# Expert gates laid out in memory by group of four expert tiles, stored in parts by SyncE from two blocks

## The reference, cut to what matters

```python
def peer(h, w_query, sub_keys, expert_u, expert_v):
    q = (hf @ w_query).reshape(T, PEER_HEADS, 2, PEER_HALF)
    scores = jnp.einsum('thcd,hcnd->thcn', q, sub_keys)
    ... # top 16 of each half, then of their sums: top_s, idx
    gates = jax.nn.softmax(top_s, axis=-1)
    u = expert_u[idx_b]
    act = jax.nn.gelu(jnp.einsum('thkd,td->thk', u, x_b))
    vv = expert_v[idx_b]
    return jnp.einsum('thk,thkd->td', g_b * act, vv)
```

## Time and profile before

| | us |
|---|---|
| median of 3 runs | 2877.3 (2871.14 to 2883.05) |
| the profiled execution | 2897.03 |
| its span, first to last instruction | 2895.3 |
| up stage with gates, about | 1000 to 1740 |
| up stage without gates, up to | 1930 |
| down stage | 1930 to 2895 |

### The profile page before, as it was taken

How to read it: one execution, slowest core, us unless ns; L and a number is a source line. 1 busy time by engine, 2 the same in 40 slices (tenths; PEclk the granted TensorE clock), 3 DMA queues, 4 the chain that set the end, 5 groups by cost and what they waited for, 6 DMA issues and landing times.

```text
span 2895.3 us, 42514 instructions
## 1 busy us (share of the span) xinstructions
PE 2689.3 (93%) x15119; PEld 2367.3 (82%) x15119; DVE 2324.9 (80%) x4258; ACT 1265.2 (44%) x2394; POOL 1077.8 (37%) x779
## 2 busy tenths in 40 slices
PE   7999776979998999999999999988999999999998
PEld 4888544768888999999999999986777777777777
DVE  3562477447889999999899776659999999999998
ACT  4211466222222499999898872222222222222222
POOL 0000000001114444444445665535555555555552
PEclk8999887989999999999999999999999999999999
DMA  6640000314348788989899999989999999999997
GB/s 225 235 169 12 10 0 16 130 73 136 114 133 281 270 313 302 340 301 329 285 330 336 378 379 370 367 303 369 377 389 388 385 384 388 363 387 389 383 376 260
DMA packets 310035, 794.35 MB, mean 274 GB/s; under 512 B 26592, under 2 KB 125568, under 8 KB 305792
## 3 DMA queue, kind: packets, MB, share of 16 engines
q0 software_dynamic: 110592, 402.70, 38.1%
q1 hardware_dynamic: 176832, 301.73, 29.6%
q10 hardware_dynamic: 22464, 88.09, 7.6%
HBM read 694.11 MB, written 98.30 MB: 274 GB/s over the span
## 4 chain that ended last, share of the span: by engine, by line
PE 36%; DVE 17%; DMA 12%; issue 9%; ACT 4%; SPq 1%; DVEq 0%; ACTq 0%
PE ps_up L392 29%; DVE row_sum L119 10%; DMA stage<-v_cols 8%; PE ps_g L439 4%; PE ps_y L802 3%; DMA expert_gate<-g_buf 2%; DMA stage<-expert_act 1%; DVE acc L856 1%; DVE coef_lo L877 1%; ACT key_distance L331 1%; DMA stage<-cols 1%; ACT v_hi L769 1%; DVE fetched L114 1%; ACT second_gate L335 1%; PE ps_g L407 1%
## 5 line engine op out<-in xcount | busy, mean ns | idle before, releaser
L96 POOL DMA_INDIRECT fetched<-u_rows,row_index x384 | 558.3, 1454 | 706.8 <-DVE row_act L114 588.5
L96 POOL DMA_INDIRECT fetched<-v_cols,row_index x384 | 515.4, 1342 | 423.4 <-DVE row_sum L119 367.8
L392 PE MATMUL ps_up<-h_hi,col_hi 128*128 128x320 f32 (+1 forms) x2288 | 555.1, 323 | 38.5 <-DVE col_lo L484 20.0
L392 PE MATMUL ps_up<-h_lo,col_hi 128*128 128x320 f32 (+1 forms) x2288 | 547.3, 320 | 0.0
L392 PE MATMUL ps_up<-h_hi,col_lo 128*128 128x320 f32 (+1 forms) x2288 | 546.7, 319 | 0.0
L114 DVE CUSTOM_DVE_ANT_0 fetched<-fetched,h_rows_then_gates 128x1024 f32<-128x1024 f32 x384 | 452.8, 1222 | 55.5 <-DMA fetched<-u_rows,row_index 42.3
L119 DVE SCALAR_TENSOR_TENSOR row_sum<-fetched,row_act,row_sum 128x1024 f32<-128x1024 f32 x381 | 486.8, 1278 | 1.5 <-DVE row_sum L119 0.5
L802 PE MATMUL ps_y<-v_hi,coef_hi 128*128 128x512 f32 x1280 | 406.0, 399 | 61.6 <-DVE coef_lo L877 57.1
L392 PEld LDWEIGHTS ps_up<-h_hi,col_hi 128*128 128x128 f32 x2288 | 387.8, 190 | 51.0 <-issue 35.2
L769 ACT ACTIVATE v_hi<-stage 128x1024 fp32r<-128x1024 f32 x128 | 135.9, 1062 | 647.9 <-DMA stage<-v_cols 638.1
L802 PE MATMUL ps_y<-v_lo,coef_hi 128*128 128x512 f32 x1280 | 400.6, 395 | 0.0
(11 more groups left out here) (245 smaller groups left out, 3487.3 us busy)
## 6 DMA issues: line engine op xcount, KB each, us to landing
stage<-cols SPq DMA_DIRECT2D x144, 512.0 KB
stage<-v_cols SPq DMA_DIRECT2D x128, 512.0 KB
expert_act<-stage ACTq DMA_DIRECT2D x128, 320.0 KB
expert_gate<-g_buf ACTq DMA_DIRECT2D x20, 2048.0 KB
stage<-expert_act SPq DMA_DIRECT2D x128, 320.0 KB
z_t<-w_ada SPq DMA_DIRECT2D x48, 512.0 KB, 6.1
g_raw<-expert_gate SPq DMA_DIRECT2D x64, 320.0 KB
h_rows_then_gates<-expert_gate SPq DMA_DIRECT2D x64, 320.0 KB
```

The source lines that it names most:

```text
L96: nc.gpsimd.indirect_dma_start(self.buf[:, n % NBUF], None, rows, bass.IndirectOffsetOnAxis(ap=self.at[:, tile, k:k + 1], axis=0)).then_in ...
L392: mm = pe.matmul(ps_up[:, b, half, 0:width], w[:, b, k], h[:, k, a:a + width], start=(k == 0 and i == 0), stop=(k == DC - 1 and i == 2))
```

## The change

`gate_d` becomes [32 groups, 128, 20 blocks, 4 tiles, 32 tokens]. A quarter's read in the down stage is now one stretch of 2560 bytes a partition, 128 pieces. A block's store writes 512 bytes at a stretch, 32 of them a partition, 4096 pieces for 2 MB.

The stores move from ScalarE's queue to SyncE's. Blocks of four groups alternate between `g_buf` and the columns of the gathered tokens in `h_hi` and `h_lo` (three blocks of 128 tokens, no longer read in the up stage), by way of plain float32 names for the same memory. A block is stored in four parts, one a slot, from the slot of its last copy on: an even block as one DMA of 512 KB a part, an odd one as three smaller DMAs a part, 12 in all. ScalarE waits for the store of the block two before, and copies a group of an odd block with two instructions of 768 and 256 elements a partition.

```diff
+GPARTS, GSTORES = 4, DC + 4
...
+        spare = [a[:, :, 0:T0] for a in h_plain]
+        A_ROWS, B_ROWS, B_K = T0 // GBLK, 8, 4
...
+            def gates_out(blk, part):
+                sp.wait_ge(g_copied, 4 * blk + 4)
+                if blk % 2 == 0:
+                    n = NGROUP // GPARTS
+                    to, src = (n * part, n), g_buf[:, GROUP * n * part:GROUP * n * (part + 1)].rearrange("p (m j) t -> p m (j t)", j=GROUP)
+                    into = gate_d[to[0]:to[0] + to[1], :, blk].rearrange("m p j t -> p m (j t)")
+                    sp.dma_start(into, src).then_inc(g_stored[0], 16)
+                else:
+                    for k in range(GSTORES * part // GPARTS, GSTORES * (part + 1) // GPARTS):
+                        rows_k, first = (A_ROWS, A_ROWS * k) if k < DC else (B_ROWS, A_TILES + B_ROWS * (k - DC))
+                        per = rows_k // GROUP
+                        src = spare[k // DC][:, k % DC, 0:rows_k * GBLK].rearrange("p (m c) -> p m c", m=per)
+                        into = gate_d[first // GROUP:first // GROUP + per, :, blk].rearrange("m p j t -> p m (j t)")
+                        sp.dma_start(into, src).then_inc(g_stored[1], 16)
...
                 g = e - LAG - 1
+                if 3 <= g < GROUPS + 3:
+                    gates_out((g - 3) // 4, (g - 3) % 4)
                 if g == GROUPS + 4:
-                    sp.wait_ge(g_stored, 16 * (GROUPS // 4))
+                    sp.wait_ge(g_stored[0], 16 * GPARTS * (GROUPS // 4 - GROUPS // 8))
+                    sp.wait_ge(g_stored[1], 16 * GSTORES * (GROUPS // 8))
...
-                elif g % 4 == 0:
-                    act.wait_ge(g_stored, 16 * (g // 4))
+                elif g % 4 == 0 and g >= 8:
+                    act.wait_ge(g_stored[g // 4 % 2], 16 * (GPARTS, GSTORES)[g // 4 % 2] * (g // 8))
                 act.wait_ge(g_done, g + 1)
...
-                nc.scalar.activation(g_buf[:, :, t0:t0 + GT], ps_g[:, g % 2].rearrange("p t n -> p n t"), ACT.Copy).then_inc(g_copied, 1)
+                if g // 4 % 2 == 0:
+                    nc.scalar.activation(g_buf[:, :, t], made, ACT.Copy).then_inc(g_copied, 1)
+                else:
+                    nc.scalar.activation(g_odd[0][:, :, :, t], made[:, 0:A_TILES].rearrange("p (k j) t -> p k j t", j=A_ROWS), ACT.Copy)
+                    nc.scalar.activation(g_odd[1][:, :, :, t], made[:, A_TILES:].rearrange("p (k j) t -> p k j t", j=B_ROWS),
+                                         ACT.Copy).then_inc(g_copied, 1)
...
-            def gates_out(blk):
-
-                act.wait_ge(g_copied, 4 * blk + 4)
-                act.dma_start(gate_d[blk], g_buf[:]).then_inc(g_stored, 16)
...
-        yield b, gate_d[b, :, bass.ds(GROUP * m, GROUP), :].rearrange("b p j t -> p b (j t)")
+        src = gate_d[bass.ds(m, 1), :, b].rearrange("o p b j t -> (o p) (b j t)")
+        yield b, src
...
-    gate_d = dram("expert_gate", (TD // GBLK, P, ETILES, GBLK))
+    gate_d = dram("expert_gate", (NGROUP, P, TD // GBLK, GROUP, GBLK))
```

More of the change, by code:

```diff
@@ L160, in loop, with route_and_up @@
     return nc.Fori(start, end, engines=[eng.engine], hint_back_edge=True)
-def route_and_up(nc, h_hi, h_lo, stage, columns, ident, cols, keys_t, v_cols, v_in, a_in, g_raw, g_in, scores, act_d, gate_d, rows):
+def route_and_up(nc, h_hi, h_lo, h_plain, stage, columns, ident, cols, keys_t, v_cols, v_in, a_in, g_raw, g_in, scores, act_d, gate_d, rows):
     with ExitStack() as ctx:
@@ L180, in route_and_up @@
         by_head = g_buf[:].rearrange("p j t -> p (j t)")
+        spare = [a[:, :, 0:T0] for a in h_plain]
+        A_ROWS, B_ROWS, B_K = T0 // GBLK, 8, 4
+        A_TILES = DC * A_ROWS
+        g_odd = (spare[0].rearrange("p k (j t) -> p k j t", t=GBLK),
+                 spare[1][:, 0:B_K, 0:B_ROWS * GBLK].rearrange("p k (j t) -> p k j t", t=GBLK))
         keys = by_head[:, 0:HC * NKEY].rearrange("p (c n) -> p c n", c=HC)
@@ L221, in route_and_up @@
         d_ready, p_ready, q_ready = sem("d_ready"), sem("p_ready"), sem("q_ready")
-        g_done, g_copied, g_stored = sem("g_done"), sem("g_copied"), sem("g_stored")
+        g_done, g_copied = sem("g_done"), sem("g_copied")
+        g_stored = [sem("g_stored0"), sem("g_stored1")]
         consts = sem("consts")
@@ L269, in _ @@
                 g = e - LAG - 1
+                if 3 <= g < GROUPS + 3:
+                    gates_out((g - 3) // 4, (g - 3) % 4)
                 if g == GROUPS + 4:
-                    sp.wait_ge(g_stored, 16 * (GROUPS // 4))
+                    sp.wait_ge(g_stored[0], 16 * GPARTS * (GROUPS // 4 - GROUPS // 8))
+                    sp.wait_ge(g_stored[1], 16 * GSTORES * (GROUPS // 8))
                     for part in gate_parts(gate_d, 0):
-                        sp.dma_start(g_raw[0][:, part[0]].rearrange("p b j t -> p b (j t)"), part[1]).then_inc(g_in[0], 16)
+                        sp.dma_start(g_raw[0][:, part[0]].rearrange("p b j t -> p (b j t)"), part[1]).then_inc(g_in[0], 16)
             sp.wait_ge(lo_done, NQ + ETILES)
@@ L314, in gates_copy @@
                     act.wait_ge(head_read, NG * HEADS)
-                elif g % 4 == 0:
-                    act.wait_ge(g_stored, 16 * (g // 4))
+                elif g % 4 == 0 and g >= 8:
+                    act.wait_ge(g_stored[g // 4 % 2], 16 * (GPARTS, GSTORES)[g // 4 % 2] * (g // 8))
                 act.wait_ge(g_done, g + 1)
-                t0 = GT * (g % 4)
-                nc.scalar.activation(g_buf[:, :, t0:t0 + GT], ps_g[:, g % 2].rearrange("p t n -> p n t"), ACT.Copy).then_inc(g_copied, 1)
+                t = slice(GT * (g % 4), GT * (g % 4) + GT)
+                made = ps_g[:, g % 2].rearrange("p t n -> p n t")
+                if g // 4 % 2 == 0:
[4 more added lines that the diff above has]
+                                         ACT.Copy).then_inc(g_copied, 1)
             def second_gates(g):
@@ L370, in _ @@
                     gates_copy(copied)
-                if 0 <= e - LAG - 1 < GROUPS and (e - LAG - 1) % 4 == 3:
-                    gates_out((e - LAG - 1) // 4)
                 act.wait_ge(up_done, n + 1)
@@ L720, in gates_in @@
                 b, src = list(gate_parts(gate_d, m + 1))[j]
-                sp.dma_start(g_raw[1 - p][:, b].rearrange("p b j t -> p b (j t)"), src).then_inc(g_in[1 - p], 16)
+                sp.dma_start(g_raw[1 - p][:, b].rearrange("p b j t -> p (b j t)"), src).then_inc(g_in[1 - p], 16)
             def load(m, j):
@@ L2049, in build @@
             sb = lambda n, s, d=F32: inner.enter_context(nc.sbuf_tensor(n, s, d))
+            h_at = [nc.sbuf_base]
             h_hi = sb("h_hi", [P, DC, S], F32R)
+            h_at.append(nc.sbuf_base)
             h_lo = sb("h_lo", [P, DC, S], F32R)
+            h_plain = [nc.alloc_sbuf_tensor_at(n, [P, DC, S], F32, offset=at) for n, at in zip(("h_hi_plain", "h_lo_plain"), h_at)]
             ident = sb("ident_f", [P, P])
@@ L2076, in build @@
             rows = Rows(nc, ctx, h_rows, t["u_rows"], t["v_cols"].rearrange("j p d -> (j p) d"))
-            route_and_up(nc, h_hi, h_lo, stage, columns, ident, t["cols"], t["keys_t"], t["v_cols"], v_in, a_in, g_raw, g_in, scores, act_d, gate_d, rows)
+            route_and_up(nc, h_hi, h_lo, h_plain, stage, columns, ident, t["cols"], t["keys_t"], t["v_cols"], v_in, a_in, g_raw, g_in, scores, act_d, gate_d, rows)
         down_and_finish(nc, stage, act_d, gate_d, t["v_cols"], v_in, a_in, g_raw, g_in, x_mid, gain2, t["out"], rows)
```

## The result

The changed kernel takes 2835.7 us (median of 4, 2833.64 to 2836.93) against 2876.77 us before (2871.14 to 2883.05): a ratio of 0.9856, 95% interval 0.9834 to 0.9878, or 41 us less. Forecast were 39 us less and 2838 us.

The account below looks back on a forecast made before the run. No engine alone sets the time; in the down stage TensorE, VectorE and DMA all stand near their limit, the full DMA engines ending last. Terms -35 - 8 - 4 + 8 = -39 us gave 2838 us, range 2812 to 2888, chance 0.47.

Parts of the forecast that it names:

- The down stage: Gate reads of 2560 bytes instead of 512 cut a tile of v to 7.05 us: -35 us, ends -12 and -50.
- The second effect: Down stage: SyncE's queue falls from 56 packets an engine and tile to 24, so loads of v wait fewer turns.
- rival B: 512-byte pieces are no dearer by themselves; down stage gains nothing, stores cost nothing: -12, 2865 us; chance 0.09.
- Slot 105: Gate reads there no longer hold SyncE's queue, so the next load of u lands in time: -8 us.
- and the same on the median: Summing step: the -39 us on the profiled 2897.0 was applied unchanged to the median 2877.3, giving 2838 us.
- The stall at 1634: TensorE's stall behind VectorE's 5.60 us wait for a fetched row during a 2 MB store goes: -4 us.
- The three stalls 147 us apart: TensorE's stalls at 1249, 1396 and 1543, 16 slots apart, the length of its loop: claimed to stay.
- The stores in 512-byte pieces: Dearer stores make slots 80 to 100 each 0.3 us too long, last slots add 2: +8 us, ends 0 and +30.
- ScalarE's wait for the store: Slots with gates: it cost 20.0 us in 10 waits, but ScalarE wins that back, so removing it gives almost nothing.
- A: Rival: the down stage falls to VectorE's floor, 6.93 us a tile: -54, 2823 us; chance 0.20.
- C: Rival: SyncE's queue is late in slots 80 to 103 alone, stalling each second slot: 49 instead of 8, 2879 us; chance 0.11.
- D: Rival: SyncE's queue is late in all 80 slots with gates, delaying loads of u: +56, 2894 us; chance 0.13.

Follow-up runs that it names:

- h_before: Kernel before, with VectorE's use of gathered rows of v done on half their columns, every DMA kept: 2868.99 us, ratio 0.9972.
- h_after: Changed kernel, with VectorE's use of gathered rows of v done on half their columns, every DMA kept: 2830.69 us, ratio 0.9837.
- q_before: Kernel before, with the down stage's gate reads issued by ScalarE instead of SyncE, same pieces and layout: 2896.6 us, ratio 1.0064.
- g_pieces: Changed kernel, but a quarter's read takes every fourth block, so 640 pieces of 512 bytes again: 2875.19 us, ratio 0.9988.
- x_layout: Kernel before with the new gate layout alone; ScalarE still stores each whole block from one g_buf: 2992.99 us, ratio 1.0392.
- c_before: The kernel before, profiled a second time without any edit: 2874.11 us (single run).
- u_unroll: Changed kernel with TensorE's loop over 16 slots with gates written out: 2829.34 us, ratio 0.9829.
- x_stores: Kernel before with the new stores alone (SyncE, two blocks, four parts), old layout, 512-byte reads: 2876.1 us, ratio 0.999.
- d_twice: Changed kernel with each part of a store sent a second time, to a tensor nobody reads: 2871.59 us, ratio 0.998.
- u_again: Changed kernel with TensorE's loop in the slots with gates written out, repeated in a second session: 2826.96 us, ratio 0.9816.

## Why the prediction was right

**The down stage (-35 us): right.** Measured 37.1 us against the second profile of before, from 952.4 to 915.3; over all profiles the stage takes 952.0 to 960.8 us with reads of 512 bytes and 915.3 to 919.3 with 2560 (h_before, h_after and q_before left out). SyncE's queue was forecast at 49 engine-us a tile, and it spends 48.5. The tile was forecast at 7.05 us in mid-stage and takes 6.96, and here the sum had luck: mid-stage tiles fell by 0.34 us (7.30 to 6.96), which over 125 tiles would be 42 us. The mean over all 127 steps fell by 0.29, from 7.18 to 6.89 us, since the tiles at the two ends of the stage gain less. A gain a tile that was too small was multiplied by too many tiles. The step that carried it, 55 against 41.8 engine-us per MB for the same bytes in 512-byte pieces, is shown by q_before, which measures 56.2 against 41.8, by g_pieces, which gave all of the gain back, and by x_layout, which had it without the new stores. The tile ended between the DMA's 7.08 and VectorE's 6.93 us, and nearer to VectorE's. The second effect, fewer packets ahead of v, isn't separated from the first: q_before removed them from that queue and gained nothing, but it delayed the gates as well. The Trainium skill ("DMA: Bandwidth & Descriptors", Specifications) has transfers run at line rate from 512 bytes, by which rival B would have come true. On full engines this case says otherwise, by 7.26 against 6.96 us a tile.

**Slot 105 (-8 us): wrong against the median.** The reasoning followed a stall of one execution. SyncE's queue was held as long in c_before, and TensorE didn't stall, so on the typical run there was nothing to gain: the stretch is 197.0 and 197.1 us, although the four reads now hold the queue for 1.79 us instead of 8.93. What failed is the step "and the same on the median".

**The stall at 1634 (-4 us): at most 1.** In c_before VectorE still waits for rows (38.7 us from 1550 to 1915), and TensorE has a stall of 1.6 us at 1662 in its place. In the changed kernel VectorE's wait for rows is 7.6 us and no such stall is left. But the stretch from the first gates to the last is only 1.0 us shorter by the first and last starts of `ps_g` shown with c_before (711.7 for 712.7 us). It was 715.8 in the first profile of before, and other profiles have 711.4 (q_before, old layout) and 714.3 (h_after, new layout), so 1 us isn't told from nothing. As at slot 105, a stall of one execution was counted for the median. The three stalls 147 us apart stayed, and are the loop's, as u_unroll shows.

**The stores in 512-byte pieces (+8 us): wrong, 0.** The surplus of packet time was forecast to stretch slots 80 to 100, and the share there did go to 1.03, but TensorE had no idle time. The failing step is the addition: I priced the rows at 41.8 engine-us per MB and the room at 1.035. In 1560 to 1700 the rows took 59.2% of 2240 engine-us for 33.64 MB, 39.4 per MB, where they had 43.1 in the same stretch of c_before. The two wrong terms, -8 and +8, cancelled, and that was luck: without the down stage the forecast had -4 us, and by the profiles the two stretches of the up stage gave 1 and the head 2, which is chance.

**ScalarE's wait for the store (about 0): right.** It fell from 20.0 to 0.9 us and the time didn't follow. x_stores, which removes it without the new layout, gained nothing.

**Rivals.** A (2823 us) asked for VectorE's floor; VectorE reached 792 of 800 us and the tile 6.96 us, so its mechanism was nearer to the truth in mid-stage than the forecast's 7.05; its total wasn't, because it took 0.40 us for each of 125 tiles and the 8 us of slot 105. C and D didn't occur: a load of u lands in 7.8 us (median), against 7.2 in c_before. d_twice shows their late loads at twice the stores.

## What to carry to other kernels

When DMA engines are full, price a transfer by the time of its pieces, not by its bytes, and move small pieces from a stage where the engines set the pace to one where TensorE does: here the same 42 MB in 512-byte pieces cost some 37 us when read and nothing that could be measured when written. A large store in small pieces is better cut into parts, since the next DMA issued behind it held its engine for 11 to 17 us; and one profiled execution isn't the median, so a stall seen once is worth profiling twice before it is counted.

## What the runs showed of the hardware that I had not expected

- A DMA's issue itself can hold an engine: 11.47 us on ScalarE for a 320 KB store behind a store of 4096 pieces, 17.05 behind the last, 195 us in 18 times in all, where the waits for the stores' own semaphore came to 2.1 us (x_layout).
- On full engines a piece of 512 bytes took 28.1 ns, 56.2 engine-us per MB, beside 41.8 for v and the activations (q_before).
- The summed packet time of a DMA queue isn't additive below full load: 45.7 engine-us per MB for the fetched rows at a share of 0.94, and 41.3 at 1.03 with twice the stores beside them, whose added pieces took 21 ns each (d_twice).
- A jump back in TensorE's loop of 16 slots costs 2.4 to 3.0 us idle in the changed kernel, and behind the first of the three, after 2.96 us idle, the 48 matmuls take 8.78 us instead of 7.04, at a granted clock of 0.87 over 1240 to 1253. Written out, the loop has neither (u_unroll, u_again).
- The changed kernel's first four runs lie within 3.3 us, those of the kernel before in the same comparison within 12.
